# Decode attention with the key blocks kept in SBUF: block sums on TensorE for the gate, and only the selected blocks scored

## The reference

```
k_full = cache_k[page_table].reshape(8, 16, 256, H, D)      # 16 blocks of 256 positions per sequence
gate   = q . mean(k_full, axis=2)                           # one number per head and block
sel    = top_k(gate, 3)                                     # the three best blocks of each head
s      = q . k(selected blocks) * scale - slope * distance  # 3 x 256 scores per head
p      = softmax([score of the new token, s])
out    = p . v(selected blocks)
```

## Time and profile before

| what | value |
|---|---|
| device time, median of 3 runs | 564.84 us (563.67 to 565.16) |
| span of the profiled execution | 562.0 us |
| PE busy | 439.0 us (78%) |
| DVE busy | 409.6 us (73%) |
| POOL busy | 283.6 us (50%) |
| mean bandwidth of the DMAs | 194 GB/s |
| mean granted PE clock | 0.857 |

### The profile page before, as it was taken

The page is one execution under the profiler, slowest core; times in us unless marked ns, Lnnn a source line. Parts: engine busy times, 40 slices in busy tenths (PEclk is TensorE's granted clock), DMA queues, the critical chain, the costliest instruction groups (busy, mean ns, idle before and its releaser), DMA issues.

```text
span 562.0 us, 6963 instructions
## 1 busy us (share of the span) xinstructions
PE 439.0 (78%) x2048; PEld 208.0 (37%) x2048; DVE 409.6 (73%) x594; ACT 141.6 (25%) x307; POOL 283.6 (50%) x266
## 2 busy tenths in 40 slices
PE   0899989969959977767295876778649883999893
PEld 0443434324334443334142633434224432444340
DVE  0458989989999986978896879684776898332133
ACT  5302002101434343144303231324130220021012
POOL 5788748876874664575433556165633632000001
PEclk9899999979997899696758596858677995999898
DMA  8986786988986887566457755274558624132101
GB/s 294 315 302 225 282 321 206 347 259 288 333 273 166 256 271 219 167 201 181 107 153 229 217 170 173 83 219 150 171 203 287 197 41 165 31 67 92 39 3 40
DMA packets 89782, 108.79 MB, mean 194 GB/s; under 512 B 60736, under 2 KB 61248, under 8 KB 89744
## 3 DMA queue, kind: packets, MB, share of 16 engines
q0 software_dynamic: 18480, 67.25, 36.5%
q1 hardware_dynamic: 59632, 23.20, 15.4%
q10 hardware_dynamic: 11632, 17.90, 9.3%
HBM read 104.02 MB, written 4.28 MB: 193 GB/s over the span
## 4 chain that ended last, share of the span: by engine, by line
PE 53%; DVE 23%; issue 10%; ACT 6%; POOL 4%; ACTq 1%; DMA 1%; DVEq 0%; POOLq 0%
PE PA L671 25%; PE PA L760 9%; DVE sall L1033 9%; DVE prod L1175 5%; PE PO L734 3%; PE SM L623 3%; ACT junk L854 2%; POOL rstd L541 2%; PE PA L711 2%; PE TP L721 2%; PE DC L772 1%; PE SM L684 1%; DMA V<-in_page_table 1%; PE DC L786 1%; DVE vn L1070 1%
## 5 line engine op out<-in xcount | busy, mean ns | idle before, releaser
L526 POOL DMA_INDIRECT K<-in_cache_k,kidx x128 | 149.1, 1164 | 78.2 <-DVE prod L1175 52.3
L671 PE MATMUL PA<-wbuf,hT 128*128 128x512 f32 x384 | 187.3, 639 | 0.0
L596 POOL TENSOR_TENSOR pprod<-K,qb 128x1024 f32<-128x1024 f32 x43 | 101.1, 2352 | 37.3 <-DVE sall L1033 36.9
L1175 DVE TENSOR_TENSOR prod<-K,qb 128x1024 f32<-128x1024 f32 x85 | 112.7, 1342 | 7.6 <-ACT qb L988 7.5
L671 PEld LDWEIGHTS PA<-wbuf,hT 128*128 128x128 f32 x384 | 75.7, 206 | 94.5 <-issue 94.3
L1033 DVE TENSOR_REDUCE sall<-prod 128x16 f32<-128x1024 f32 x85 | 100.9, 1206 | 0.0
L540 POOL TENSOR_SCALAR rstd<-msum 128x1 f32<-128x1 f32 (+3 forms) x25 | 6.5, 261 | 148.5 <-ACT junk L854 77.0
L760 PE MATMUL PA<-wbuf,hT 128*128 128x512 f32 x128 | 60.1, 624 | 0.0
L1033 DVE TENSOR_REDUCE sall<-pprod 128x16 f32<-128x1024 f32 x43 | 51.9, 1208 | 1.2 <-POOL pprod L596 1.2
L950 ACT ACTIVATE pr<-pr,smax 128x128 f32<-128x128 f32 (+3 forms) x32 | 18.0, 562 | 134.7 <-DVE smax L1125 129.6
L711 PE MATMUL PA<-kT,qT 64*128 64x128 f32 (+3 forms) x64 | 28.9, 536 | 11.2 <-ACT vn L917 7.3
(11 more groups left out here) (177 smaller groups left out, 462.7 us busy)
## 6 DMA issues: line engine op xcount, KB each, us to landing
V<-in_cache_v SPq DMA_DIRECT2D x366, 32.0 KB
wbuf<-in_w_in ACTq DMA_DIRECT2D x5, 2048.0 KB, 11.8
wbuf<-in_w_in SPq DMA_DIRECT2D x2, 2048.0 KB, 13.7
wbuf<-in_w_out ACTq DMA_DIRECT2D x2, 2048.0 KB, 8.4
K<-in_cache_k,kidx POOLq DMA_INDIRECT x128, 5.6
ya<-in_x_prompt SPq DMA_DIRECT2D x2, 512.0 KB, 4.6
yb<-in_x_prompt SPq DMA_DIRECT2D x2, 512.0 KB, 8.1
out<-yb SPq DMA_DIRECT2D x4, 256.0 KB
```

The source lines that it names most:

```text
L526: pool.indirect_dma_start(K[:, m % SLOTS, :, :].rearrange("p r w -> p (r w)"), None, k_rows, bass.IndirectOffsetOnAxis(ap=kidx[:, b, n:n + ...
L596: pool.tensor_tensor(pprod[:, :, :], K[:, m % SLOTS, :, :], qb[:, b % 2, :].unsqueeze(1).broadcast_to([P, 2, W]), ALU.mult).then_inc(s_pmu ...
L671: last = pe.matmul(PA[n % 2][:, :], lhs, rhs, start=(kc == 0), stop=(kc == KC - 1))
L1175: dve.tensor_tensor(prod[:, slot, :, :], K[:, m % SLOTS, :, :], qb[:, b % 2, :].unsqueeze(1).broadcast_to([P, 2, W]), ALU.mult).then_inc(s ...
```

## The change

The ring of ten slots becomes a resident set of 16 slots, one for each block of a sequence (`K`, 64 KB of each partition). Blocks are no longer multiplied one by one. Instead the two rows of a block in each partition are added (`sum_rows`, half of the elements of the old product): five of the 16 blocks by DVE, 11 by POOL, into a ring of six `ksum` buffers. PE sums four such blocks at a time over the partitions with a window of ones (step `gs`, four steps a sequence, four matmuls each, into the new PSUM bank `GB`). Step `ga`: DVE multiplies these sums with the query, reduces, transposes, and picks the three best blocks. Step `pg` finds the pages. Step `ex`, in four parts: DVE loads eight block numbers at a time into registers and multiplies only the selected blocks, 24 small products at addresses that come from registers (128 partitions by 128 elements). Step `sr` reduces all 24 at once. `bc` broadcasts only the block numbers now, and the one-hot products are gone.

The first five loads of the next sequence are issued by POOL only after the last product of the sequence before (`s_ext`), and each later load is issued five blocks ahead, at a step `ks`. The query has one buffer in place of two. Values have one buffer in place of two, fetched and used in two halves of four heads (`pv0`, `pv1`); the registers are loaded four at a time from a transposed tile `selT`. The small results of a sequence are gathered after each sequence, not at the end. The list of steps has new due times, and the DMA ring of POOL is 2048 in place of 4096.

```diff
-SLOTS = 10
-POOL_SHARE = 3
+SUMS = 6
+PARTS = 4
+LEAD = 5
+def of_dve(n):
+
+    return n % 3 == 1
...
-START_US, PERIOD_US = 1.24, 39.0
-
-GT, BC, FV, MT, MB, QB, PVD = 2.44, 5.68, 9.0, 17.16, 28.24, 18.41, 53.07
+END_US, PERIOD_US, ARRIVE_US = 38.0, 43.0, 1.5
+GS, GA, PG, EX, EX_STEP, SR, BC = 1.5, 3.0, 4.6, 4.5, 1.8, 13.0, 15.0
+MT, MB, PV0, PV1, QB, FV = 20.0, 26.0, 32.0, 52.0, 14.0, 9.0
 FIN = 3.8
-SP_HEADS, SP_LAST = 8, 5
+ACT_RANKS = (1, 2)
...
+        def sum_rows(eng, b, n, done):
+
+            eng.wait_ge(s_k[n], 16 * (b + 1))
+            if n < SUMS and b >= 1:
+                eng.wait_ge(s_scr, b)
...
+            if n >= SUMS:
+                eng.wait_ge(s_gs, G * b + (n - SUMS) // 4 + 1)
+            eng.tensor_tensor(ksum[:, n % SUMS, :], K[:, n, 0, :], K[:, n, 1, :], ALU.add).then_inc(done, 1)
...
+                if s[0] == "ex" and s[2] == PARTS - 1 and s[1] < B - 1:
+                    pool.wait_ge(s_ext, s[1] + 1)
+                    for n in range(LEAD):
+                        load_k(NB * (s[1] + 1) + n)
                 if s[0] == "ks":
                     b, n = s[1], s[2]
...
+                    if not of_dve(n):
+                        sum_rows(pool, b, n, s_psum)
+                    if b >= 1 and n + LEAD < NB:
+                        load_k(NB * b + n + LEAD)
...
+                elif kind == "gs":
+                    b, g = s[1], s[2]
+                    pe.wait_ge(s_psum, pool_sums(NB * b + 4 * g + 4))
+                    pe.wait_ge(s_dsum, dve_sums(NB * b + 4 * g + 4))
+                    if g == 0 and b >= 1:
+                        pe.wait_ge(s_gate, b)
+                    for j in range(4):
+                        last = pe.matmul(GB[32 * j:32 * j + 32, :], win[:, 31 - g:63 - g],
+                                         ksum[:, (4 * g + j) % SUMS, :], start=(g == 0), stop=(g == G - 1),
+                                         tile_position=(0, 32 * j))
+                    last.then_inc(s_gs, 1)
...
+                elif kind == "ga":
                     b = s[1]
...
+                    dve.wait_ge(s_gs, G * (b + 1))
+                    dve.wait_ge(dc_free, dc_use[("qb", b)] + 1)
+                    dve.tensor_tensor(sumq, GB[:, :], qb[:, :], ALU.mult).then_inc(s_gate, 1)
+                    dve.wait_ge(s_gate, b + 1)
+                    link(dve.tensor_reduce(g128[:, 0:H], sumq.rearrange("p (h d) -> p h d", h=H), AX.X, ALU.add))
+                    link(dve.transpose(gT[:, :], g128[:, :]))
+                    for j in range(4):
+                        last = dve.tensor_copy(g16[:, :, j], gT[32 * j:32 * j + H, 0:G])
+                    link(last)
+                    gates = g16[:, :, :].rearrange("h g j -> h (g j)")
+                    link(dve.max(top8[:, :], gates))
+                    link(dve.max_index(topi[:, :], top8[:, :], gates))
...
+                elif kind == "ex":
+                    b, part = s[1], s[2]
+                    if part >= 1:
+                        dve.wait_ge(s_sel, b + 1)
+                    size = H * TOP // PARTS
+                    for x in range(size * part, size * (part + 1)):
+                        k, h = divmod(x, H)
+                        if h == 0:
+                            block_regs = [dve.alloc_register(f"blk{b}_{k}_{i}") for i in range(H)]
+                            dve.load(block_regs, selT[k:k + 1, b % 2, 0:H])
+                        n = dve.snap(block_regs[h], min_val=0, max_val=NB - 1)
+                        last = dve.tensor_tensor(kq[:, h * TOP + k, :, :],
+                                                 K[:, bass.ds(n, 1), :, h * HD:(h + 1) * HD]
+                                                 .rearrange("p a r d -> p (a r) d"),
+                                                 qb[:, h * HD:(h + 1) * HD].unsqueeze(1).broadcast_to([P, 2, HD]),
+                                                 ALU.mult)
...
+                    if part == PARTS - 1:
+                        last.then_inc(s_ext, 1)
+                elif kind == "sr":
+                    b = s[1]
+                    dve.wait_ge(s_ext, b + 1)
+                    if b >= 1:
+                        dve.wait_ge(s_pex, b)
+                    dve.tensor_reduce(sc[:, :, :, :].rearrange("p h k r -> p (h k) r"), kq[:, :, :, :], AX.X,
+                                      ALU.add).then_inc(s_scr, 1)
```

More of the change, by code:

```diff
@@ L49, with dve_sums, pool_sums, act_ranks @@
 COL = {"u": 0, "va": 1, "ga": 2, "q": 3, "k": 4, "v": 5, "gb": 6}
-SLOTS = 10
-POOL_SHARE = 3
-def of_pool(m):
-    return m % POOL_SHARE == 1
-def pool_count(m):
-    return sum(map(of_pool, range(m)))
-def sp_heads(b):
-    return SP_HEADS if b < B - 1 else SP_LAST
+SUMS = 6
[3 more added lines that the diff above has]
+    return n % 3 == 1
+def dve_sums(m):
+    return sum(of_dve(x % NB) for x in range(m))
+def pool_sums(m):
+    return m - dve_sums(m)
+def act_ranks(b, hh):
+    return ACT_RANKS if (b, hh) == (B - 1, 1) else ()
 def make_schedule():
@@ L567, in _ @@
             pool.memset(osb[:, :, :], 0.0).then_inc(s_const, 1)
-            for n in range(4, SLOTS - 1):
+            for n in range(4, NB):
                 load_k(n)
@@ L1253, in _ @@
                                       ).then_inc(dc_free, 1)
-                elif kind == "pvd":
+                elif kind == "pv0":
                     b = s[1]
```

342 lines of the change are left out of this document (152 added, 190 removed).

## The result

The changed kernel takes 614.5 us (median; 611.6 to 618.0) against 565.0 for the kernel before (563.7 to 568.4): ratio 1.085, 95% interval 1.079 to 1.091. The direction was forecast, the size was not: 579 was predicted, and the upper end of the range was 612.

The account below looks back on a forecast made before the run. It took PE as the base with DVE taking turns, and a selection-and-key-load loop as the new pace: first gate 73, seven cycles 399, tail 104, 576 us of span, 2.8 more for device time: 579, range 522 to 612.

Parts of the forecast that it names:

- First gate and tail: Time to the first gate matmul, 73 us, and time after the last one, 104 us.
- the wait of 5 us at `mt`: PE's wait for the selection maximum at mt, up to 5 us; 5 us of it added to the tail.
- the late cycle: Four cycles with the prompt's attention and gated steps: 59 us each, where 67 were needed before.
- The three early cycles: Two cycles of 53.6 us and one of 56, where an early cycle needed 44 before.
- the prompt's share: Prompt attention and gated steps between the parts of ex on DVE, 4 us added to a late cycle.
- The first half of the loop: Last gs to s_ext on DVE (gate, pages, products): 15.6 us, bounds 12.6 to 27, with no key DMA running.
- The second half: s_ext to the next last gs on POOL and DMAs: 38 us, from limits of 35 and 42.
- the burst: POOL requesting 16 key blocks in 27.3 us, 308 GB/s; weights and values might collide with it and delay the keys.
- DVE below 300 us: Sign that the forecast is right: DVE's busy time falls below 300 us, from about 410.
- The supply-bound rival: Weights and values collide with key bursts: cycles 58 early, 63.5 late, 613 us; chance 0.15.
- The short loop: Faster products and block landings, SP's 48 us sets the cycle, 50 with the prompt: 525 us; chance 0.35 with nearby cases.
- The 5 us a cycle for engines that lock each other out: DVE and POOL blocking each other, up to 0.7 us per POOL sum step in the second half; left out.

Follow-up runs that it names:

- e1: Changed kernel with the rstd steps that DVE consumes made on DVE, square root left out: 586.6 us, 1.032 of the kernel before.
- e2: Kernel before with the rstd steps that DVE consumes made on DVE, square root left out: 543.9 us, ratio 0.959.
- e18: Changed kernel with rstd made on DVE including its square root, nine small operations: 608.1 us, 1.075 of the kernel before.
- e11: Changed kernel with row sums of blocks 4 to 15 and three of four gs steps cut to 16 of 512 columns: 580.5 us, 1.025.
- e9: Changed kernel with the first half of the values (pv0) due at 44 us instead of 32: 614.1 us, 1.088 of the kernel before.
- e14: Changed kernel with all row sums and rstd (no square root) moved from POOL to DVE: 611.2 us, 1.080 of the kernel before.
- e7: Changed kernel with blocks due 2.0 us apart instead of 1.5, and gs, ga, pg, ex 3 us later: 631.1 us, 1.112.
- e4: Changed kernel whose next key loads wait only for the last row sum; products read a constant tile: 607.4 us, 1.073.
- e13: Changed kernel with every row sum made by DVE, none by POOL: 614.9 us, 1.090 of the kernel before.
- e5: Changed kernel with three of four gs steps summing 128 of 512 columns on PE, row sums whole: 600.1 us, 1.057.

## Why the prediction was right and wrong, by its steps

First gate and tail: right in their numbers. The last `gs` of the first sequence ended at 71.3 (forecast 73), and 105.3 us stood behind the last one (104). In the tail there was luck: the wait of 5 us at `mt` that stands in its sum did not come, and one of 7.3 us at the transposes ahead of an output tile (L753) did, for `hT` of DVE, where the kernel before had 1.9.

The step that failed is the late cycle. The three early cycles were to take 163 us (53.6 twice and 56) and took 162.3; the four late ones were to take 236 (59 each) and took 272.7, and these 37 us are the whole error of 36 in the time. The forecast had a late cycle as an early one plus 5.5 (4 for the prompt's share, 1.5 for `rstd`); measured it is 68.2 on average, 14.1 above the early average of 54.1. That the early sum came out is luck too, since it is made of two errors that cancel, as follows.

The first half of the loop was too dear. From the last `gs` to the end of the products it took 12.1, 11.4 and 11.8 us early (15.6 forecast) and 12.8 to 15.4 late (19.6 with the prompt's share). The 192 products had 286 ns each (300 taken), but they overlap: 41.7 us of busy time make 0.22 apiece, so that 24 of them take 5.2 us, not 7.2. The gate took 3.4 us to the first `selT` (3.6 taken), the pages 1.3 (1.8), and a register load 0.6, not 1.0.

The second half failed. It took 42.1, 46.5 and 38.4 us early (38 forecast) and 55.5, 57.1, 56.3 and 49.0 late (39.5, the `rstd` term included). Its terms were each somewhat short: a POOL sum 1.31 us for 1.2, a load 1.01 for 0.94, a key block 7.1 from issue to landing for 5.6, a DVE sum 1.07 for 0.68, and 44.4 us of `gs` for 30 (1.39 a step where 0.95 was read off a full-speed row: a step took 1.06 us at a granted clock of 1.00 and 1.7 to 1.9 at 0.50 to 0.58, in early cycles too). Added up they come to about the early excess of 4 us. The late 10 to 18 us are more than these sizes. The runs speak for a wrong form: I took the late cycle as the early loop plus a surcharge, while it is a chain through gated tiles, `rstd`, products, loads and sums that wait for one another in list order. With `rstd` made on DVE without its root the four late cycles lose 24 us, 5.9 each, where 1.5 was taken (e1; in the kernel before, e2, they lose 19); the small steps of the root put back 19 of them (e18), and their 1.1 to 1.4 us at each of 20 places cost 22 us in both kernels; light sums take 23 us off the same four cycles (e11), where the forecast had all but PE's share of the sums hidden. The kernel before had that chain too: its late cycles were 67.2, 65.8 and 70.5 us, and the changed kernel's 68.4, 72.5 and 70.0 are no shorter. The forecast had taken 8 us off them because DVE's 265 us went; the trace of before already said that those cycles were not DVE's alone (DVE 54.5 of 67 us, PE 41.9).

The early cycles were forecast to grow from 44 to 53.6, and then 56, and came out at 54, 58 and 50: right in kind. When ACT evacuates the prompt's projection tiles, the changed kernel is 13 us behind at the last value tile, 31 at the last `u` tile and 36 at the first gated one, and 49.7 at the end, so some seven tenths of the loss have come by 255 us. At the fourth gate it is 19 us behind: the new list has the gates at other places among the tiles.

`mt`: PE was to wait up to 5 us for its maximum there. The waits at DC for `sbias` and `mx` were 5.7 us in the whole run. What stood there instead was not in the sum at all: the first half of the values, 17.9 us, landing 11.5 and 14.3 us after issue beside the key burst. The forecast had named the burst as a danger for the keys, not for what shares the DMA engines with them. In time it was worth nothing alone (e9), and it may well have eaten e14's gain.

DVE below 300 us: right (253.4), and without effect. That was the forecast's own point, as to the early cycles.

The supply-bound rival gave 613 and the result was 614.5, but by another mechanism: its cycles were 58 and 63.5, and half of the bytes gave 13 us, not 90. The short loop had its products right (0.21 taken, 0.22 measured; a first half of 12.6 taken, 11.4 to 12.1 measured) and fell with the rest. The 5 us a cycle for engines that lock each other out were rightly left out of POOL's half: its sum took 0.1 us more than forecast, and a load right behind one 0.95 to 1.24 us between 83 and 112 us, not 1.78; it was DVE that was slowed.

Of the 49.5 us the runs put about 34 on the added sums (14 on half of the matmuls' work, 20 mostly on the row sums), 6 to 7 on `rstd`'s way over POOL, and 7 to 13 on keys that can't stream. These shares were taken one by one and overlap; how they add was not tried, and that one chain through all engines makes the rest is argued from the traces. Not settled is why e7's wider spacing costs 17 us; by its trace they lie in the early cycles (177.2 us in three, 162.3 in the kernel after). Whether sums in a buffer of their own would help e4, and what a second buffer of values would give, wasn't tried.

## What to carry to other kernels

When engines walk one common list, work taken from an engine is worth only what of it stood in the chain, and work added to another costs in part even if both look idle: test it by adding a known small cost at the suspected place in both kernels and see whether it comes back whole. Run each "fix" on the kernel before as well; 22 of the 28 us that e1 found were no part of the change. A burst that starts sooner makes what shares its DMA engines later, so look at the other transfers before you call it a gain. And cut a trace into its stages before you read "no change" as "no effect".

## What the runs showed of the hardware

A DVE add of two SBUF operands, 128x512, took 1069 ns while POOL made sums of the same kind, and 684 ns once POOL made none (e13):

```profile
L427 DVE TENSOR_TENSOR ksum<-K 128x512 f32<-128x512 f32 x128 | 83.1, 684 | 66.0 <-PE GB L789 41.0 <-DMA K<-in_cache_k,kidx 25.0
```

That is 0.385 us on each of 40 sums, 15 us of DVE. The Trainium skill, "SBUF — State Buffer", section "Who interferes with whom", says that a DVE instruction with two SBUF inputs contends with a GpSimd instruction that reads SBUF. The rows agree; the forecast had left it out.

Register loads: SP's load of four registers for the values took 0.30 us (the L408 piece above), where six took 0.71 to 1.27 in the earlier trace rows. The Trainium skill, "DMA: Bandwidth & Descriptors", section "Latency and other measured facts", has a floor of about 600 ns; the measurement decides, and for four registers it is half of that. DVE's loads of eight took 0.60 (L1220, median 597 ns).

Products at a register address showed no surcharge: 286 ns for 128x128, where the line between the fixed-address rows gives 0.29; one after another they came every 0.22 us.

PE's sums shrink with their columns, but not in proportion. The groups above mix shapes; kept apart, the 192 of 256 matmul records that were narrowed are these, with 128 columns (e5) and with 16 (e11):

```profile
L790 PE MATMUL GB<-ksum,win 128*32 128x128 f32 x192 | 11.7, 319 | 28.2 <-POOL ksum L427 17.6 <-DVE ksum L427 10.7
L791 PE MATMUL GB<-ksum,win 128*32 128x16 f32 x192 | 6.7, 205 | 10.6 <-POOL ksum L428 10.5
```

Three quarters of the 44.4 us at 512 columns are 33. A quarter of the columns left 11.7 us of them, and a thirty-second left 6.7. What the rest at few columns is made of was not tried.
